# The first weights of an f32 transformer kernel: input in halves, a chain of half-sized weight transfers, constant products around the first transposes

## Chip, cores and metric

One core of one Trainium2 chip runs the whole program. The metric is the device time of the kernel in microseconds (us), the median of several executions. Everything is f32.

## What is computed

Two blocks in sequence on x, 256 tokens by 1024 features. The first block has two hybrid layers. Each of them begins with a gated feed-forward layer on the normed input, and only this beginning matters here:

```python
def rmsnorm(x, g):
    xf = x.astype(jnp.float32)
    y = xf * lax.rsqrt(jnp.mean(xf * xf, axis=-1, keepdims=True) + EPS)
    return (y * g.astype(jnp.float32)).astype(x.dtype)

def swiglu(x, w_gu, w_down):
    gate, up = jnp.split(x @ w_gu, 2, axis=-1)
    return (jax.nn.silu(gate) * up) @ w_down
```

with D_MODEL = 1024 and D_FF = 2816. After it come a mixer (a gated recurrence, windowed attention, spatial gating), a second feed-forward layer and a gated projection of p; then the same again for layer two. The second block has a short convolution, latent attention and two mixture-of-experts layers with 64 experts, whose weights are read from HBM as well. All weights are used once, 617 MB of reads in all.

## The kernel before

The program is written out by hand, one instruction stream per engine, with semaphores between them. Names that the steps below touch:

- **Weights.** `ring` has four slots of 3.1 MB in SBUF. A feed-forward layer is cut into 11 units of 256 hidden columns; unit u uses slot u % 4. One unit is three transfers of 1 MB, issued on SyncE's queue by `load` (line 1684): the gate part and the up part (`ffn_gate_up`, both 128 partitions x 8 pieces x 256 columns) and the down part (`ffn_down`). Each of them adds 16 to `unit_loaded[slot]`. Before it issues, `load` waits for `unit_free[slot]`. The first unit is issued by `load_first` (lines 1687 and 1688), without a wait; its down part counts on `final_loaded`, a semaphore of much later loads that is borrowed here. The queue's order is: two small tables (`const`, `gT1`), x (line 1678, into `h`), unit 0, units 1, 2 and 3, and then one unit each time a slot comes free.
- **Other queues.** ScalarE's queue issues ten small loads, and the second part of `const` (784 KB, line 1979) behind its first evictions. GpSimd issues nine loads (`rows`, `sgw` and others, lines 1768 to 1774; 2.53 MB) behind its first power, which follows the squares of x.
- **TensorE.** In order: a transpose of the gains (line 2649); `h_turn`, 16 transposes of x (line 2333), after a wait for all of x; a transpose of `gT2` (line 2656), the gains and convolution weights of the second block; a wait for the evictions (`h_copied`); then `ffn`. `gate_up` (line 2362) makes 128 hidden columns for all tokens in 16 products of 256 columns, eight with gate weights and eight with up weights, and waits once per unit (`loaded`, line 2349: all three parts, for unit 0 the two first). `spread` (line 2345) sets the statistics of the norm into PSUM after the first 128 columns. `down` (line 2372) is four products of 512 columns. In the profile each f32 product is two records.
- **ScalarE and VectorE.** `h_copied` evicts the transposed x with its gain: twelve activations (line 1803) and one VectorE product (line 2054). ScalarE then squares x (line 1808), VectorE and GpSimd make the reciprocal root, and VectorE multiplies each gate and up result by it (lines 2075 and 2076), ScalarE does the silu, VectorE the product (`hidden_ready`).
- `S_mla`, five semaphores, counts the loads of the latent attention in the second block. TensorE waits there for the counts in `MLA_LOADS` (line 590).

Of the kernel before, what the change touches and what calls it, by code (L numbers as in the profile page):

```python
# [27 lines left out]
P = 128  # L28
# [142 lines left out]
class Semaphores:  # L171

    def __init__(self, sem):
        self.const_loaded = sem("const_loaded")
        self.small_loaded = sem("small_loaded")
        self.h_loaded = sem("h_loaded")
        self.gl_ready = sem("gl_ready")
        self.h_half = sem("h_half")
# [81 lines left out]
        self.mla_pv = sem("mla_pv")  # L261
        self.mla_out = sem("mla_out")
        self.mla_lat_copied = sem("mla_lat_copied")
# [29 lines left out]
def build(nc, A, out):  # L293

    ctx = ExitStack()
    with ctx:
# [3 lines left out]
        S = Semaphores(lambda name: ctx.enter_context(nc.semaphore(name)))  # L300
# [5 lines left out]
        h = sb("h", [P, 3, D])  # L306
# [282 lines left out]

        MLA_LOADS = [2, 2, 2, 3, 4]  # L590

# [1083 lines left out]
        def _(sp):  # L1675
            sp.dma_start(const[:, 0:CONST_FIRST], A["const_table"][:, 0:CONST_FIRST]).then_inc(S.const_loaded, 16)
            sp.dma_start(gT1[:, :], A["norm_gains"].rearrange("l n (k c) -> (l n k) c", c=P)).then_inc(S.const_loaded, 16)
            sp.dma_start(h[:, 0:2, :], x_in).then_inc(S.h_loaded, 16)

# [6 lines left out]
            def load_first(parts):  # L1686
                for (dst, src), counted in zip(parts, (unit_loaded[0], unit_loaded[0], S.final_loaded)):
                    sp.dma_start(dst, src).then_inc(counted, 16)

# [634 lines left out]
        def _(pe):  # L2324
            mm = nc.tensor.matmul

            def h_turn(q):

                for t in range(2):
                    for n in range(2):  # L2330
                        pe.wait_ge(S.h_half, 4 * q + 2 * t + n + 1)
                        for k in range(4):
                            last = nc.tensor.transpose(PS[:, 2 * t + n, k * P:(k + 1) * P],
                                                       h[:, t, (4 * n + k) * P:(4 * n + k + 1) * P], ident)
                        last.then_inc(S.h_turned, 1)
# [12 lines left out]
            def loaded(use, slot):  # L2348
                pe.wait_ge(unit_loaded[slot], 48 * use + (48 if slot else 32))

            def ffn(l, m, u0, n, with_p=False):
                def gate_up(f, local):

                    unit = u0 + local // 2
                    slot = unit % SLOTS
                    w = ring[:, slot, 0:4096].rearrange("p (s k f) -> p s k f", s=2, k=KD)
                    j = local % 2
                    if j == 0:
                        loaded(USES * l + f[0] + unit // SLOTS, slot)
                    for s in range(2):  # L2360
                        for k in range(KD):
                            last = mm(PS[:, 4 + local % 4, s * 256:(s + 1) * 256], lhsT=w[:, s, k, j * P:(j + 1) * P],  # L2362
                                      rhs=xT[:, k, META:T2], start=k == 0, stop=k == KD - 1)
                            if s == k == 0 and j == 1 and local > 1:

                                last.then_inc(unit_free[(unit - 1) % SLOTS], 1)
                    last.then_inc(S.gateup_done, 1)
# [15 lines left out]
                gate_up([0], 0)  # L2383
                spread(n, 0)
                gate_up([0], 1)
                if m == 0:
# [263 lines left out]
            for l in range(DEPTH):  # L2650
                if l == 0:
                    pe.wait_ge(S.h_loaded, 16)
                h_turn(4 * l)
                if l == 0:
                    pe.wait_ge(S.small_loaded, SMALL_LOADS)
                    nc.tensor.transpose(PS[:, 7, 0:n_rows2], gT2[0:n_rows2, :], ident[0:n_rows2, 0:n_rows2]).then_inc(S.rowsT_done, 1)
                h_copied(4 * l)
# [36 lines left out]
```

## Time and profile before

| | us |
|---|---|
| median of 3 executions | 2574.58 |
| lowest, highest | 2574.37, 2577.57 |
| profiled execution | 2573.37 |
| its span | 2571.5 |
| TensorE busy | 2413.5 (94% of the span) |
| VectorE busy | 695.3 |
| ScalarE busy | 341.8 |
| mean granted TensorE clock | 0.979 of full speed |
| HBM traffic | 616.89 MB read, 240 GB/s over the span |

The profile is of one execution. The span runs from the first instruction to the last, and the execution's own time is 1.9 us longer. A row of a timeline has the start, the time that a merged group of instructions took, the engine, the line in the kernel, output and input, the count, and in brackets the idle time before it with what ended it. "SPq" is SyncE as an issuer of DMAs; the time in such a row is the time the issuing took, not that of the transfer. A granted clock of 1.00 is 2.4 GHz and one of 0.50 is 1.2 GHz.

### The profile page before, as it was taken

```text
span 2571.5 us, 29601 instructions
## 1 busy us (share of the span) xinstructions
PE 2413.5 (94%) x11424; PEld 1464.8 (57%) x11424; DVE 695.3 (27%) x1575; ACT 341.8 (13%) x829; POOL 48.2 (2%) x95
## 2 busy tenths in 40 slices
PE   8999999999999999999999988988989998989887
PEld 6776647775677655777576533444437553444432
DVE  1112631112211263111222432333333343233233
ACT  1101230002100123000210200000012220000001
POOL 2000000000100000000000000000000000000000
PEclk9999999999999999999999999999999999999999
DMA  9443334433644243343282399999992259999997
GB/s 318 147 148 113 128 104 161 147 119 114 236 156 160 92 148 113 135 161 131 86 301 118 131 403 422 422 422 422 422 402 101 82 237 409 422 422 422 422 422 304
DMA packets 205207, 618.88 MB, mean 241 GB/s; under 512 B 15005, under 2 KB 120294, under 8 KB 155734
## 3 DMA queue, kind: packets, MB, share of 16 engines
q1 hardware_dynamic: 198080, 610.25, 61.3%
q0 software_dynamic: 1600, 5.06, 0.6%
q10 hardware_dynamic: 5462, 2.67, 0.4%
q8 instruction: 45, 0.74, 0.1%
q14 instruction: 20, 0.16, 0.0%
HBM read 616.89 MB, written 1.05 MB: 240 GB/s over the span
## 4 chain that ended last, share of the span: by engine, by line
PE 67%; DMA 24%; DVE 3%; SPq 2%; issue 1%; ACT 1%; DVEq 0%; POOL 0%; POOLq 0%; ACTq 0%
DMA ring<-expert_parts 23%; PE PS L2362 23%; PE PS L2372 11%; PE PS L1643 6%; PE PS L1550 4%; PE PS L2414 3%; PE PS L2449 3%; PE PS L1600 2%; PE PS L2599 2%; PE PS L1620 2%; SPq L1042 2%; PE PS L2431 1%; PE PS L758 1%; PE PS L1156 1%; PE PS L623 1%
## 5 line engine op out<-in xcount | busy, mean ns | idle before, releaser
L2362 PE MATMUL PS<-xT,ring 128*128 128x256 f32 x2816 | 627.2, 381 | 7.0 <-DMA ring<-ffn_gate_up 2.9
L2362 PEld LDWEIGHTS PS<-xT,ring 128*128 128x128 f32 x2816 | 537.6, 191 | 116.1 <-issue 41.0
L1643 PE MATMUL PS<-ring,arena 128*32 128x512 f32 x2048 | 264.5, 661 | 72.8 <-DMA ring<-expert_parts 72.8
L2372 PE MATMUL PS<-ring,arena 128*128 128x512 f32 x704 | 315.9, 592 | 0.0
L1600 PE MATMUL PS<-arena,xn 128*128 128x128 f32 (+1 forms) x1536 | 271.4, 306 | 4.3 <-DVE arena L1359 4.3
L1600 PEld LDWEIGHTS PS<-arena,xn 128*128 128x128 f32 (+1 forms) x1536 | 215.4, 189 | 90.7 <-issue 31.7
L2075 DVE TENSOR_TENSOR arena<-PS,rb 128x256 f32<-128x256 f32 x88 | 37.4, 425 | 728.8 <-PE PS L2362 728.6
L1643 PEld LDWEIGHTS PS<-ring,arena 128*32 128x32 f32 x2048 | 75.4, 120 | 251.2 <-issue 251.0
L2372 PEld LDWEIGHTS PS<-ring,arena 128*128 128x128 f32 x704 | 133.5, 190 | 132.6 <-issue 126.8
L1460 DVE TENSOR_TENSOR h<-h,PS 128x1024 f32<-128x1024 f32 (+1 forms) x96 | 116.8, 1217 | 323.4 <-PE PS L1620 323.4
L1620 PE MATMUL PS<-arena 128*128 128x512 f32 (+1 forms) x404 | 198.5, 615 | 5.3 <-DVE h L1460 5.3
L1825 ACT ACTIVATE arena<-arena 128x256 f32<-128x256 f32 x88 | 36.6, 416 | 804.7 <-DVE arena L2075 804.6
L1663 PE MATMUL PS<-ring,arena 128*32 128x512 f32 x1024 | 118.2, 602 | 24.3 <-ACT arena L1281 24.3
L1620 PEld LDWEIGHTS PS<-arena 128*128 128x128 f32 (+1 forms) x404 | 56.6, 160 | 103.2 <-issue 85.5
L1550 PE MATMUL PS<-xT,ring 128*128 128x272 f32 x384 | 90.7, 398 | 1.6 <-ACT xT L1087 0.8
L2449 PE MATMUL PS<-ring,xT 128*128 128x512 f32 x192 | 87.7, 603 | 0.0
L1550 PEld LDWEIGHTS PS<-xT,ring 128*128 128x128 f32 x384 | 73.5, 193 | 18.2 <-issue 2.0
L1663 PEld LDWEIGHTS PS<-ring,arena 128*32 128x32 f32 x1024 | 30.3, 110 | 86.3 <-issue 58.8
L2414 PE MATMUL PS<-ring,xT 128*128 128x512 f32 (+1 forms) x192 | 69.6, 522 | 0.2
L1280 ACT ACTIVATE arena<-PS 128x272 f32<-128x272 f32 x32 | 12.7, 398 | 428.5 <-PE PS L1633 428.5
L1515 DVE TENSOR_TENSOR arena<-arena,PS 128x256 f32<-128x256 f32 x32 | 13.4, 420 | 184.7 <-ACT arena L1278 184.7
L1451 DVE TENSOR_SCALAR arena<-rows,arena 128x128 f32<-128x128 f32 x96 | 32.9, 343 | 107.8 <-ACT arena L1284 104.4
(381 smaller groups left out, 1707.2 us busy)
## 6 DMA issues: line engine op xcount, KB each, us to landing
ring<-expert_parts SPq DMA_DIRECT2D x384, 1024.0 KB, 15.1
ring<-ffn_gate_up SPq DMA_DIRECT2D x88, 1024.0 KB, 7.7
ring<-ffn_down SPq DMA_DIRECT2D x44, 1024.0 KB, 9.8
ring<-w_in SPq DMA_DIRECT2D x16, 768.0 KB, 5.8
ring<-conv_w_in SPq DMA_DIRECT2D x12, 1024.0 KB, 12.0
ring<-w_out_rows SPq DMA_DIRECT2D x8, 768.0 KB, 6.3
ring<-ple_gate SPq DMA_DIRECT2D x8, 768.0 KB, 6.2
rows<-norm_gains POOLq DMA_DIRECT2D x8, 512.0 KB, 8.9
```

The lines of the kernel that those rows point to most:

```text
L1042: return sp.dma_start(ring[:, j, PART * n:PART * (n + 1)], src[:, n].rearrange("o p w -> p (o w)"))
L1460: v_.tensor_tensor(tile2(h[0:w, t, :]), tile2(h[0:w, t, :]), PS[0:w, 6:8, :], ALU.add).then_inc(M[i].added, 1)
L1550: last = mm(PS[:, 3 * b + s, 0:T2], lhsT=w[:, s, k, j * P:(j + 1) * P], rhs=xT[:, k, :], start=k == 0, stop=k == KD - 1)
L1600: last = mm(PS[:, half, (k % HALF) * P:(k % HALF + 1) * P], lhsT=xn[0:w, t, k * P:(k + 1) * P], rhs=onehot[0:w, t, :], start=t == 0, stop= ...
L1620: last = mm(PS[0:w, bank + c, :], lhsT=weightsT[:, P * t:P * t + w], rhs=ysb[:, c * 512:(c + 1) * 512], start=True, stop=True)
L1643: last = mm(PS[BLK * j:BLK * (j + 1), 2, :], lhsT=xgT[:, k, j * BLK:(j + 1) * BLK], rhs=gu[j][:, k, :], start=k == 0, stop=k == KD - 1)
L1663: last = mm(PS[BLK * j:BLK * (j + 1), 4 + n, :], lhsT=hidT[:, f, j * BLK:(j + 1) * BLK], rhs=w[:, f, n * 512:(n + 1) * 512], start=f == 0, ...
L2362: last = mm(PS[:, 4 + local % 4, s * 256:(s + 1) * 256], lhsT=w[:, s, k, j * P:(j + 1) * P], rhs=xT[:, k, META:T2], start=k == 0, stop=k = ...
L2372: return mm(PS[:, 2 * t + n, :], lhsT=hid[:, j, t * P:(t + 1) * P], rhs=w[:, j, n * 512:(n + 1) * 512], start=first, stop=final, skip_grou ...
L2414: last = mm(PS[:, bank, at:at + width], lhsT=src[:, k, xcol(t)], rhs=w[:, k, 0:width], start=k == 0, stop=k == kk - 1)
L2449: last = mm(PS[:, bank, :], lhsT=xT[:, k, xcol(t)], rhs=wu[:, k, :], start=k == 0, stop=k == KD - 1)
L2599: last = mm(PS[:, 2 * t + n, :], lhsT=xT[:, k, xcol(t)], rhs=wo[:, k, :], start=k == 2, stop=k == 7)
```

## The change

x is sent as two transfers, one for each 128 tokens, with a semaphore each (`h_loaded`, `h_second`). TensorE waits for each half before its eight transposes.

The gate and up weights of the first unit are sent as four transfers of 512 KB (four of the eight pieces of the contraction each). The first is issued when the first half of x has landed, the second when the second half has, and each further one when the last but one has landed, so two of them (1 MB) are under way. The unit's down part is issued when the third quarter has landed, and unit 1 after the fourth. TensorE waits for each quarter before the products that read it, in place of one wait for gate and up. The four quarters count on four of the `S_mla` semaphores, and the counts in `MLA_LOADS` are raised to match. An unused semaphore goes.

`first_warm(2)` sets two products of a constant with the identity, whose results nobody reads, ahead of the transposes of x, and two more behind them. The transpose of `gT2` moves from ahead of the first products to behind `spread`.

```diff
-        MLA_LOADS = [2, 2, 2, 3, 4]
+        MLA_LOADS = [3, 3, 3, 4, 4]
...
-            sp.dma_start(h[:, 0:2, :], x_in).then_inc(S.h_loaded, 16)
+            sp.dma_start(h[:, 0:1, :], x_in[:, 0:1, :]).then_inc(S.h_loaded, 16)
+            sp.dma_start(h[:, 1:2, :], x_in[:, 1:2, :]).then_inc(S.h_second, 16)
...
             def load_first(parts):
-                for (dst, src), counted in zip(parts, (unit_loaded[0], unit_loaded[0], S.final_loaded)):
-                    sp.dma_start(dst, src).then_inc(counted, 16)
+
+                (gate, gate_src), (up, up_src), (dn, dn_src) = parts
+                sp.wait_ge(S.h_loaded, 16)
+                sp.dma_start(gate[:, 0:4], gate_src[:, 0:4]).then_inc(S_mla[0], 16)
+                sp.wait_ge(S.h_second, 16)
+                sp.dma_start(gate[:, 4:8], gate_src[:, 4:8]).then_inc(S_mla[1], 16)
+                sp.wait_ge(S_mla[0], 16)
+                sp.dma_start(up[:, 0:4], up_src[:, 0:4]).then_inc(S_mla[2], 16)
+                sp.wait_ge(S_mla[1], 16)
+                sp.dma_start(up[:, 4:8], up_src[:, 4:8]).then_inc(S_mla[3], 16)
+                sp.wait_ge(S_mla[2], 16)
+                sp.dma_start(dn, dn_src).then_inc(S.final_loaded, 16)
+                sp.wait_ge(S_mla[3], 16)
...
+            def first_warm(n):
+
+                for _ in range(n):
+                    mm(PS[:, 5, 0:2 * P], lhsT=ident, rhs=const[:, 0:2 * P], start=True, stop=True)
+
             def h_turn(q):
 
                 for t in range(2):
+                    if q == 0:
+                        pe.wait_ge(S.h_second if t else S.h_loaded, 16)
...
-                pe.wait_ge(unit_loaded[slot], 48 * use + (48 if slot else 32))
+                pe.wait_ge(unit_loaded[slot], 48 * use + (48 if slot else 0))
...
-                    if j == 0:
+                    if j == 0 and (m or local):
                         loaded(USES * l + f[0] + unit // SLOTS, slot)
                     for s in range(2):
                         for k in range(KD):
+                            if m == local == 0 and k in (0, 4):
+                                pe.wait_ge(S_mla[2 * s + k // 4], 16)
...
                 gate_up([0], 0)
                 spread(n, 0)
+                if m == 0:
+                    pe.wait_ge(S.small_loaded, SMALL_LOADS)
+                    nc.tensor.transpose(PS[:, 7, 0:n_rows2], gT2[0:n_rows2, :], ident[0:n_rows2, 0:n_rows2]).then_inc(S.rowsT_done, 1)
...
                 if l == 0:
-                    pe.wait_ge(S.h_loaded, 16)
+                    first_warm(2)
                 h_turn(4 * l)
                 if l == 0:
-                    pe.wait_ge(S.small_loaded, SMALL_LOADS)
-                    nc.tensor.transpose(PS[:, 7, 0:n_rows2], gT2[0:n_rows2, :], ident[0:n_rows2, 0:n_rows2]).then_inc(S.rowsT_done, 1)
+                    first_warm(2)
                 h_copied(4 * l)
```

How the instructions stand on SyncE's queue at the start of the program, before (`mla_loaded0` to `3` are the first four of `S_mla`):

```order
L1676 DMA const<-const_table 128x264
L1677 DMA gT<-norm_gains 128x128
L1678 DMA h<-x 128x2x1024
L1688 DMA ring<-ffn_gate_up 128x8x256 x2
L1688 DMA ring<-ffn_down 128x2x1024
L1684 DMA ring<-ffn_gate_up 128x8x256 [waits unit_free1]
L1684 DMA ring<-ffn_gate_up 128x8x256
```

and in the changed kernel:

```order
L1678 DMA h<-x 128x1024
L1679 DMA h<-x 128x1024
L1691 DMA ring<-ffn_gate_up 128x4x256 [waits h_loaded]
L1693 DMA ring<-ffn_gate_up 128x4x256 [waits h_second]
L1695 DMA ring<-ffn_gate_up 128x4x256 [waits mla_loaded0]
L1697 DMA ring<-ffn_gate_up 128x4x256 [waits mla_loaded1]
L1699 DMA ring<-ffn_down 128x2x1024 [waits mla_loaded2]
L1685 DMA ring<-ffn_gate_up 128x8x256 [waits unit_free1,mla_loaded3]
L1685 DMA ring<-ffn_gate_up 128x8x256
```

Unit 0's gate and up parts have become four issues, each behind a landing, and unit 1 has moved behind the landing of the last of them. Before, nothing on this queue waited for a landing.

TensorE from the transposes of x to unit 1, before:

```order
L2333 MATMUL PS<-const,h 128x128 x3
L2656 MATMUL PS<-const,gT 128x73 [waits small_loaded]
L2362 MATMUL PS<-xT,ring 128x256 [waits unit_loaded0,xT_vec,xT_act]
L2362 MATMUL PS<-xT,ring 128x256 x15
L2345 MATMUL PS<-diag,const 128x128 [waits diag_ready]
L2345 MATMUL PS<-diag,const 128x128
L2362 MATMUL PS<-xT,ring 128x256 x16
L2372 MATMUL PS<-ring,arena 128x512 [waits hidden_ready,final_loaded]
```

and in the changed kernel:

```order
L2342 MATMUL PS<-const 128x256 x2
L2383 MATMUL PS<-xT,ring 128x256 [waits mla_loaded0,xT_vec,xT_act]
L2383 MATMUL PS<-xT,ring 128x256 x3
L2383 MATMUL PS<-xT,ring 128x256 [waits mla_loaded1]
L2383 MATMUL PS<-xT,ring 128x256 x3
L2383 MATMUL PS<-xT,ring 128x256 [waits mla_loaded2]
L2383 MATMUL PS<-xT,ring 128x256 x3
L2383 MATMUL PS<-xT,ring 128x256 [waits mla_loaded3]
L2383 MATMUL PS<-xT,ring 128x256 x3
L2364 MATMUL PS<-diag,const 128x128 [waits diag_ready]
L2364 MATMUL PS<-diag,const 128x128
L2408 MATMUL PS<-const,gT 128x73 [waits small_loaded]
```

The 16 products of the first 128 columns have four waits instead of one, the transpose of `gT2` (128x73) stands behind the statistics instead of ahead of the products, and two constant products stand where it was.

## Rows read from the trace of the kernel before

**Rows 1.** Timeline of TensorE, start of the program

```profile
7.03 3.67 PE L2333 MATMUL PS<-const,h 128*128 128x128 f32 x16 [3.07 <-DMA h<-x]
10.50 0.33 PE L2656 MATMUL PS<-const,gT 73*128 73x73 f32 x1
13.74 8.83 PE L2362 MATMUL PS<-xT,ring 128*128 128x256 f32 x32 [2.91 <-DMA ring<-ffn_gate_up]
22.41 0.61 PE L2345 MATMUL PS<-diag,const 128*128 128x128 f32 x4
...
29.76 3.60 PE L2372 MATMUL PS<-ring,arena 128*128 128x512 f32 x8
34.91 7.17 PE L2362 MATMUL PS<-xT,ring 128*128 128x256 f32 x32 [1.55 <-DMA ring<-ffn_down]
...
45.35 7.07 PE L2362 MATMUL PS<-xT,ring 128*128 128x256 f32 x32
```

**Rows 2.** Timeline of SyncE's queue: x, units 0, 1 and 2

```profile
1.64 0.43 SPq L1678 DMA_DIRECT2D h<-x  x1
2.11 1.09 SPq L1688 DMA_DIRECT2D ring<-ffn_gate_up  x2
...
7.07 6.05 SPq L1684 DMA_DIRECT2D ring<-ffn_gate_up  x2
13.16 4.75 SPq L1684 DMA_DIRECT2D ring<-ffn_down  x1
...
31.09 3.74 SPq L1684 DMA_DIRECT2D ring<-ffn_down  x1
```

**Rows 3.** Single DMAs issued at 0.72, 1.64, 2.62, 7.07, 13.16, 31.09: us to landing

```profile
const<-const_table SPq DMA_DIRECT2D x1, 132.0 KB, 2.3
...
h<-x SPq DMA_DIRECT2D x1, 1024.0 KB, 5.3
...
ring<-ffn_gate_up SPq DMA_DIRECT2D x1, 1024.0 KB, 11.0
...
ring<-ffn_gate_up SPq DMA_DIRECT2D x1, 1024.0 KB, 20.2
...
ring<-ffn_down SPq DMA_DIRECT2D x1, 1024.0 KB, 21.7
...
ring<-ffn_down SPq DMA_DIRECT2D x1, 1024.0 KB, 12.4
```

**Rows 4.** Chain of work that ended last, 0 to 200 us, in order of time

```profile
42.08 3.43 PE PS L2372 x8
45.52 6.91 PE PS L2362 x32
```

**Rows 5.** Stretches: length, busy PE, PEld, DVE, ACT, POOL, granted clock, DMA share, GB/s

```profile
0.00:7.00 7.00, 0.48 (x1) 0.18 (x1) 0.35 (x2) 1.28 (x1) 0.19 (x4) 1.00 0.74 217
7.00:16.00 9.00, 6.06 (x25) 5.40 (x26) 1.34 (x4) 5.28 (x16) 2.18 (x4) 0.93 1.08 364
16.00:34.90 18.90, 17.36 (x70) 13.27 (x68) 3.13 (x9) 0.83 (x2) 7.41 (x18) 0.94 1.05 364
```

**Rows 6.** DMA queues of GpSimd (q0) and ScalarE (q10), 0 to 60 us: packets, MB, share

```profile
q0 software_dynamic: 800, 2.53, 12.2%
q10 hardware_dynamic: 582, 0.91, 4.2%
```

**Rows 7.** Timeline of VectorE, its eviction of x

```profile
10.74 0.69 DVE L2054 TENSOR_TENSOR xT<-PS,gT 128x512 f32<-128x512 f32 x1 [6.45 <-PE PS L2333]
```

**Rows 8.** Stretches with the clock down, and one after the wait of 1.55 us

```profile
14.80:18.20 3.40, 3.40 (x10) 2.65 (x9) 0.24 (x2) 0.00 (x0) 3.40 (x6) 0.50 1.01 387
35.00:45.00 10.00, 10.00 (x40) 7.50 (x41) 1.18 (x3) 0.42 (x1) 6.32 (x19) 1.00 1.08 364
653.10:659.90 6.80, 6.08 (x14) 4.88 (x15) 1.39 (x4) 3.76 (x7) 4.04 (x7) 0.50 1.07 374
```

**Rows 9.** Timeline of TensorE, start of the second layer

```profile
651.67 1.32 PE L2333 MATMUL PS<-const,h 128*128 128x128 f32 x8 [2.50 <-DVE h L2035]
```

More of the change, by code:

```diff
@@ L177, in __init__ @@
         self.h_loaded = sem("h_loaded")
+        self.h_second = sem("h_second")
         self.gl_ready = sem("gl_ready")
@@ L261, in __init__ @@
         self.mla_pv = sem("mla_pv")
-        self.mla_out = sem("mla_out")
         self.mla_lat_copied = sem("mla_lat_copied")
```

## The prediction

> **What bounds the kernel now.** I read the engines' shares of the span first (in the table above), then TensorE's timeline of the first 60 us with SyncE's queue beside it, the landing times of single DMAs, the bytes moved in stretches, and last the stretches in which the clock was down. TensorE is busy 94% of the span. From 34.91 us on it runs a beat of 6.91 + 3.43 = 10.34 us per 128 hidden columns without a stop [rows 1, 4]. So a shift of 34.91 reaches the end of the program one for one, and a shift of anything earlier counts only as far as it moves 34.91. What sets it?
>
> TensorE starts unit 0 at 13.74, when the up weights have landed (issued near 2.6, 11.0 us under way), works until 29.76 + 3.60 = 33.36, and then stands 1.55 us for unit 1's third part: issued at 13.16, 21.7 us under way, landed at 34.87 [rows 1 to 3]. That landing is a matter of bytes, not of when it was asked for. Up to 34.9 us the engines moved 1.52 + 3.28 + 6.88 = 11.68 MB, with a DMA share of 1.05 to 1.08 in the last two stretches [rows 5]. SyncE's queue had to bring 0.2 (tables) + 1.05 (x) + 3.15 (unit 0) + 3.15 (unit 1) = 7.54 MB; beside it run 2.53 MB of GpSimd's queue and 0.91 of ScalarE's [rows 6], which the change leaves as they are. That makes 10.98 MB; the other 0.7 belong to unit 2, queued behind. Unit 2 lands at 31.09 + 12.4 = 43.5 and is wanted at 45.35 + 10.34 = 55.7 [rows 1 to 4]. Only unit 1 binds.
>
> **The new start, part by part.** x as a whole takes 5.3 us from 1.64 [rows 2, 3]; its second half is 0.52 MB, 1.4 us at 364 GB/s [rows 5], so the first half lands at about 5.5, the second at 6.9. A link of the new chain (0.52 MB, asked for when an earlier one has landed) isn't in this trace. The row below it is 132 KB in 2.3 us, the row above it the 5.3 us of x [rows 3]. I take 3.6: the 2.3 us, less 0.2 for its own 135 KB, plus 1.4 for 0.52 MB at 364 GB/s, and 0.1 for the queue to wake, since with 1 MB under way little stands ahead of a link. Then gate's halves land at 9.1 and 10.5, up's at 12.7 and 14.1, and unit 1 is first asked for at about 14.2 instead of 7.07 [rows 2].
>
> TensorE: the 16 transposes (3.67 us) run from 5.5 to 9.2. The evictions end 4.4 us after the first transpose, as now (7.03 to 10.74 + 0.69 [rows 1, 7]), at 9.9. Of the four constant products, 0.43 us each (6.91 us for 16 of that width [rows 4]), the first two lie in the wait for x and the other two beside the evictions, ending at 10.1; without those covers they would cost 1.7 us. Then 1.7 us of products per half: gate until 13.5, up's first half until 15.2, the second until 16.9. The statistics (0.61 us) and the moved transpose (0.33) make 17.9 [rows 1], the second 128 columns 24.8, the down products 28.2. With the clock down as long as now (3.4 us at half [rows 8], 1.7 us lost) it is 29.9. **TensorE is ready for unit 1 at 28.2 to 29.9**, 3.5 to 5.2 us before 33.36. Unit 0's down part, asked for at 12.8, is wanted at 24.8. If it takes the 20.2 us of unit 1's first part [rows 3] it lands at 33.0, and TensorE is ready at 36.4, 1.1 us after unit 1; with x's 5.3 us it costs nothing. I take nothing, since its bytes stand ahead of all of unit 1's; 1.1 us is a bound. VectorE's wait for the moved transpose is 0.3 us; behind it stands only the first hidden block, covered by 6.9 us of products. The counts in the later loads follow the reused semaphores: nothing.
>
> **What it is worth is decided at unit 1.** Its landing needs the same 10.98 MB. Asking in small pieces can't bring them sooner on full engines; it can only leave gaps. By 14.2 us SyncE's queue has brought 3.35 MB and ScalarE's 0.91. Unit 0's down part is then just starting and GpSimd's rows start about 1.5 us sooner than now (their issue follows the squares of x), so I put 4.65 MB at 16 us against 4.80 [rows 5]. The 0.15 MB missing are 0.4 us at 364 GB/s: **unit 1 at 35.3, +0.4**. Lower end: the 0.7 MB of unit 2 no longer run ahead, -1.9. Upper end: each link takes 5.3 us, two pairs of them put unit 1's request 3.4 us later, and little fills the gap: +2.9.
>
> TensorE will then stand 5 to 7 us before unit 1, where it stood 1.55. After that 1.55 us the clock stayed at 2.4 GHz (35 to 45 at 1.00). After the stand from 10.8 to 13.74 it was at 1.2 GHz from 14.8 to 18.2; at 650, after a stand of 2.50 us and another short one, from 653.1 to 659.9 [rows 1, 8, 9]. Half of 3.4 and of 6.8 us is lost, 1.7 or 3.4 us. Here nothing later hides it, since unit 2 has 12 us to spare. Bounds are 0 and 3.4. A stand of 5 to 7 us is like the rows with a fall, and dense work after it like the one at 14.8, so I take 2.0. The fall that now lies at 14.8 gives nothing back where it is avoided: what it delays ends at 33.36, ahead of unit 1.
>
> Sum: +0.4 + 2.0 = **+2.4 us**. The profiled execution took 2573.37 us and would take 2575.8. It lies 1.2 us under the median of the three, 2574.58, so the forecast for a median is **2577.0**. A measurement of this kernel can tell about 0.2%, 5.1 us, from no change.
>
> A rule speaks against halves. The Trainium skill (DMA: Bandwidth & Descriptors, Rules for kernel authors) asks for at least 1 MiB per DMA, and its table in Bandwidth has 341 GB/s at 1 MB and 138 at 64 KB. By it I estimate some 300 GB/s for 512 KB, 0.3 us more per link and so +0.6 on the sum. No run shows it yet.
>
> **Rivals.**
> (a) *The wait eats the gain and nothing else happens*: the clock stays up; 0 to +0.8 us, 2574.6 to 2575.4. For it: the 1.55 us without a fall. Against: the stand is three times that. 15%.
> (b) *Fewer bytes of unit 2 run ahead*, as unit 1's parts are asked for close together: up to -1.9 us, 2572.7. Against: the queue is as deep as now by then. 8%.
> (c) *The early start goes through*: unit 1 gets ahead of GpSimd's 2.53 MB and TensorE goes on at 28.2 to 29.9, 5.0 to 6.7 us sooner, 2567.9 to 2569.6. It decides if unit 1 lands by 29.8. With all the bytes that takes 6.3 MB in 13.8 us, 459 GB/s where the row has 364 [rows 5]. 3%.
> (d) *The chain starves the engines*, the slower side: links at 5.3 us, because the 0.91 MB of ScalarE's queue and GpSimd's rows come in between while SyncE's queue holds only 1 MB; unit 1 at 37.8, the clock down for 6.8 us: +2.9 + 3.4 = +6.3, 2580.9. It passes 5.1 us when unit 1 lands after 36.6 with the long fall. Under way beside GpSimd's rows a part took 20.2 us [rows 3], which speaks for it; that ScalarE's table is small, against. 12%. The Trainium skill (DMA: Bandwidth & Descriptors, Queues, rings and completion order) says that the engines go round robin between queues, by which a short queue would lose its share.
> (e) *x's halves don't land apart*, both at 6.9: TensorE's start moves by 1.4 us, unit 1 by some 0.4. Inside the forecast's range.
>
> **How the numbers follow.** The forecast with (e) has 62%, 2575 to 2579. The range of 8 in 10 takes in (a), most of (b) and the shorter end of (d): 2573.0 to 2580.4. Faster by over 0.2%: (c) and little else, 4%. Slower by over 0.2%: three quarters of (d), 9%. Within: 87%.
>
> **What would show it.** Right: first products of unit 0 near 10 us and the last of its first up products near 17; one wait of over 4 us that a DMA of unit 1 ends at 35 to 36; a granted clock of 0.50 for some us behind it; 11.7 MB moved by then; the beat of 10.34 us as before. Wrong: no long wait before unit 1, or its landing before 33.5; a clock of 1.00 after it. A DMA share well under 1 between 7 and 15 us would speak for (d).

## The result, and the profile after

The change made the kernel slower: 2583.12 us against 2574.47 us, medians of 16 executions each. The ratio is 1.0031 with an interval of 1.0020 to 1.0042, +5.1 to +10.8 us. I had forecast 2577.0, at most 2580.4, and had given 9% to slower by over 0.2%. A second measurement of the same kernel, below, has 2581.48 against 2576.44, ratio 1.0023 (1.0009 to 1.0037). A ratio is not the quotient of the two medians beside it and can differ from it by 0.001. One of the 35 executions of the kernel before beside e9 to e12 took 8001.73 us at a mean granted clock of 0.305 and is left out of the ratios (the median without it is 2576.26).

The profiled execution took 2584.11 us, span 2582.3. TensorE's timeline of its start, against [rows 1]:

```profile
6.91 3.67 PE L2352 MATMUL PS<-const,h 128*128 128x128 f32 x16 [1.25 <-DMA h<-x]
...
11.74 3.62 PE L2383 MATMUL PS<-xT,ring 128*128 128x256 f32 x16
17.53 5.41 PE L2383 MATMUL PS<-xT,ring 128*128 128x256 f32 x16 [2.17 <-DMA ring<-ffn_gate_up]
...
30.24 3.60 PE L2393 MATMUL PS<-ring,arena 128*128 128x512 f32 x8
38.77 8.80 PE L2383 MATMUL PS<-xT,ring 128*128 128x256 f32 x32 [4.94 <-DMA ring<-ffn_down]
...
50.84 7.07 PE L2383 MATMUL PS<-xT,ring 128*128 128x256 f32 x32
```

The transposes start 0.12 us sooner than before, not 1.5. The gate products begin at 11.74, two us sooner than 13.74, but the up products only at 17.53, and TensorE is ready for unit 1 at 33.84, later than the 33.36 of before. Unit 1 lands at 38.7 instead of 34.9. The first 32 records behind it take 8.80 us instead of 7.17.

SyncE's queue in the same profile, against [rows 2]:

```profile
1.64 0.42 SPq L1678 DMA_DIRECT2D h<-x  x1
2.10 0.43 SPq L1679 DMA_DIRECT2D h<-x  x1
6.89 0.38 SPq L1691 DMA_DIRECT2D ring<-ffn_gate_up  x1
8.19 0.38 SPq L1693 DMA_DIRECT2D ring<-ffn_gate_up  x1
10.42 0.37 SPq L1695 DMA_DIRECT2D ring<-ffn_gate_up  x1
13.06 0.37 SPq L1697 DMA_DIRECT2D ring<-ffn_gate_up  x1
17.50 0.37 SPq L1699 DMA_DIRECT2D ring<-ffn_down  x1
18.88 5.42 SPq L1685 DMA_DIRECT2D ring<-ffn_gate_up  x2
24.34 5.78 SPq L1685 DMA_DIRECT2D ring<-ffn_down  x1
```

Each issue from 6.89 to 18.88 follows a landing. The first half of x landed after 5.2 us, about as long as the whole of x took [rows 3]; the second after 6.1. Single DMAs of the chain, issued at 6.89, 8.19, 10.42 and 13.06, with KB and us to landing:

```profile
ring<-ffn_gate_up SPq DMA_DIRECT2D x1, 512.0 KB, 3.5
...
ring<-ffn_gate_up SPq DMA_DIRECT2D x1, 512.0 KB, 4.8
...
ring<-ffn_gate_up SPq DMA_DIRECT2D x1, 512.0 KB, 7.1
...
ring<-ffn_gate_up SPq DMA_DIRECT2D x1, 512.0 KB, 5.8
```

I had put every link (one transfer of the chain, from issue to landing) at 3.6. The stretches, with the columns of [rows 5], then two single microseconds and the stretch behind unit 1's landing:

```profile
0.00:7.00 7.00, 2.27 (x6) 1.38 (x7) 0.35 (x2) 1.28 (x1) 0.19 (x4) 1.00 0.64 189
7.00:16.00 9.00, 8.36 (x36) 7.36 (x36) 1.34 (x4) 5.28 (x16) 2.31 (x4) 1.00 0.85 261
16.00:34.90 18.90, 16.30 (x61) 12.29 (x61) 3.10 (x9) 0.83 (x2) 6.89 (x16) 0.91 1.04 348
6.00:7.00 1.00, 0.09 (x1) 0.09 (x2) 0.00 (x0) 0.00 (x0) 0.00 (x0) 1.00 0.39 119
7.00:8.00 1.00, 1.00 (x5) 1.00 (x6) 0.00 (x0) 0.00 (x0) 0.00 (x0) 1.00 0.11 34
38.90:42.10 3.20, 3.20 (x8) 2.57 (x9) 0.00 (x0) 0.00 (x0) 2.42 (x8) 0.50 1.10 353
```

By 16 us 1.32 + 2.35 = 3.67 MB have moved, where it was 4.80 [rows 5]. The 1.13 MB missing are 3.1 us at 364 GB/s, and the stretch to 34.9 runs at 348 instead of 364 GB/s, 0.3 MB or 0.8 us more. Together that is the 3.9 us by which unit 1 is late. Counted up to the start of unit 1's products, both kernels have moved the same 11.67 MB, 8.22 of them on SyncE's queue, before by 34.9 us and now by 38.7. Between 6 and 8 us the DMA engines are nearly idle: x's halves land at 6.9 and 8.2, and until the first of them nothing new is asked for. Against the 364 and 378 GB/s of before these two microseconds account for 0.59 of the 1.13 MB; the rest is missing from 8 to 16 us, where 289 GB/s stand against 362. Then the clock is at 1.2 GHz behind the stand (TensorE's wait ahead of unit 1), which costs 1.6 us.

So 5.5 us of the 10.8 between the spans of the two profiled executions arise in the first 50 us, and they stay. The first transposes after the first feed-forward layer, of the kernel before and of the changed one:

```profile
246.04 1.32 PE L2333 MATMUL PS<-const,h 128*128 128x128 f32 x8 [0.63 <-DVE h L2035]
```

```profile
251.53 1.32 PE L2352 MATMUL PS<-const,h 128*128 128x128 f32 x8 [0.63 <-DVE h L2047]
```

I call this time the mark; it contains the whole start and little else. The rest of the 10.8, 5.3 us, comes far behind the change. In both kernels the clock falls where the first expert layer begins, but for 10 us in the profile of before and 20 in that of the changed kernel:

```profile
1458.70:1468.80 10.10, 10.10 (x28) 6.50 (x26) 0.91 (x2) 0.00 (x0) 0.00 (x0) 0.50 1.01 423
```

```profile
1465.50:1485.90 20.40, 20.21 (x52) 11.69 (x51) 2.64 (x3) 0.16 (x1) 0.00 (x0) 0.50 0.64 266
```

Whether the change causes that too was the second question for the runs.

### The profile page after: what moved, and what is told of

It reads as the page before. It is cut to its first block, busy times and chain, and to the rows that moved or that the text cites. A ratio compares the mean times of both kernels' runs of the same rounds, so it can differ in the third digit from the quotient of the medians.

```text
span 2582.3 us, 29622 instructions
## 1 busy us (share of the span) xinstructions
PE 2422.9 (94%) x11432; PEld 1470.4 (57%) x11432; DVE 695.3 (27%) x1575; ACT 341.5 (13%) x829; POOL 48.1 (2%) x95
## 4 chain that ended last, share of the span: by engine, by line
PE 67%; DMA 24%; DVE 3%; SPq 2%; issue 1%; ACT 1%; DVEq 0%; POOL 0%; POOLq 0%; ACTq 0%
DMA ring<-expert_parts 23%; PE PS L2383 23%; PE PS L2393 11%; PE PS L1643 6%; PE PS L1550 4%; PE PS L2438 3%; PE PS L2473 3%; PE PS L1600 2%; PE PS L2623 2%; PE PS L1620 2%; SPq L1042 2%; PE PS L758 1%; PE PS L2455 1%; PE PS L1156 1%; PE PS L623 1%
## 5 line engine op out<-in xcount | busy, mean ns | idle before, releaser
L1837 ACT ACTIVATE arena<-arena 128x256 f32<-128x256 f32 x88 | 36.6, 416 | 809.1 <-DVE arena L2087 809.1
```

## The experiments

The twelve runs fall into three groups, e1 to e4, e5 to e8 and e9 to e12. Each group ran on one chip with the kernel before beside it: 12 executions of each kernel (10 of e2, e5 and e6), 35 of the kernel before. A version with a second number repeats an earlier one. In the table "asked" is the issue of unit 1's first part, "unit 1" the start of its products, "stand" TensorE's wait ahead of it, "rest" the span behind the mark, all from the run's one profile. Where "stand" is 0, unit 1 had landed before TensorE was ready.

| run | asked | unit 1 | stand | mark | rest | median, before | ratio (interval) |
|---|---|---|---|---|---|---|---|
| before | 7.07 | 34.91 | 1.55 | 246.04 | 2325.5 | | |
| changed | 18.88 | 38.77 | 4.94 | 251.53 | 2330.8 | 2583.12, 2574.47 | 1.0031 (1.0020, 1.0042) |
| e1 no chain | 7.42 | 35.33 | 6.48 | 248.24 | 2326.0 | 2576.68, 2576.15 | 1.0012 (0.9995, 1.0028) |
| e2 tail free | 13.98 | 39.12 | 4.46 | 251.69 | 2323.4 | 2577.66, 2576.15 | 1.0015 (0.9999, 1.0032) |
| e3 constants in the stand | 18.80 | 38.86 | 2.52 | 249.99 | 2326.9 | 2579.89, 2576.15 | 1.0011 (0.9995, 1.0027) |
| e4 GpSimd's loads late | 17.80 | 31.34 | 0.25 | 242.47 | 2322.3 | 2570.72, 2576.15 | 0.9976 (0.9962, 0.9989) |
| e5 table late | 16.83 | 39.45 | 9.70 | 252.78 | 2320.8 | 2582.19, 2574.80 | 1.0027 (1.0007, 1.0046) |
| e6 three under way | 12.92 | 37.22 | 7.08 | 250.77 | 2321.0 | 2578.03, 2574.80 | 1.0010 (0.9992, 1.0028) |
| e7 before, loads late | 9.16 | 35.05 | 0 | 246.07 | 2332.9 | 2574.49, 2574.80 | 1.0002 (0.9986, 1.0018) |
| e8 no chain, loads late | 7.79 | 29.83 | 0 | 240.85 | 2331.9 | 2573.36, 2574.80 | 0.9990 (0.9972, 1.0007) |
| e9 changed, again | 20.54 | 38.75 | 4.00 | 252.28 | 2320.9 | 2581.48, 2576.44 | 1.0023 (1.0009, 1.0037) |
| e10 no constants | 21.30 | 38.71 | 4.49 | 251.22 | 2333.1 | 2581.38, 2576.44 | 1.0025 (1.0008, 1.0043) |
| e11 as e4, again | 18.79 | 33.66 | 0 | 244.68 | 2327.5 | 2573.98, 2576.44 | 0.9985 (0.9970, 1.0001) |
| e12 no chain, both late | 7.65 | 28.60 | 0 | 239.62 | 2322.8 | 2566.59, 2576.44 | 0.9963 (0.9949, 0.9977) |

**e1: without the chain.** All six waits of `load_first` go; halves, constants and the moved transpose stay.

```diff
-                sp.wait_ge(S.h_loaded, 16)
                 sp.dma_start(gate[:, 0:4], gate_src[:, 0:4]).then_inc(S_mla[0], 16)
-                sp.wait_ge(S.h_second, 16)
                 sp.dma_start(gate[:, 4:8], gate_src[:, 4:8]).then_inc(S_mla[1], 16)
-                sp.wait_ge(S_mla[0], 16)
...
```

> The changed kernel with all six waits of the SyncE queue in the first unit's load taken away: x in halves, gate and up in halves, the constant products and the moved transpose stay, and the waits of TensorE for each quarter. Theory 1 (the chain leaves the DMA engines short of work: 3.67 MB moved by 16 us instead of 4.80, so unit 1 lands 3.9 us later, and the longer stand before it costs a fall of the clock): 4.7 to 4.8 MB by 16 us, unit 1 lands at 34.5 to 35.3, TensorE ready before 33, no or a short stand, 2572 to 2576. Theory 2 (the added products, the moved transpose or the many small pieces cost, not the waits): unit 1 still lands after 37 or the time stays above 2580.

Its stretches and TensorE's timeline:

```profile
0.00:7.00 7.00, 3.33 (x11) 2.44 (x12) 0.36 (x2) 1.28 (x1) 0.19 (x4) 1.00 0.70 224
7.00:16.00 9.00, 8.32 (x41) 6.79 (x39) 1.34 (x4) 5.28 (x16) 3.37 (x6) 1.00 1.08 361
16.00:34.90 18.90, 12.85 (x53) 9.55 (x53) 3.10 (x9) 0.83 (x2) 6.51 (x17) 0.93 1.05 364
```

```profile
5.84 3.12 PE L2346 MATMUL PS<-const,h 128*128 128x128 f32 x16 [0.21 <-DMA h<-x]
...
25.25 3.60 PE L2387 MATMUL PS<-ring,arena 128*128 128x512 f32 x8
35.33 8.96 PE L2377 MATMUL PS<-xT,ring 128*128 128x256 f32 x32 [6.48 <-DMA ring<-ffn_down]
```

4.82 MB by 16 us, as before (4.80), and unit 1 at 35.3. Theory 1 holds for the bytes and the landing: the waits made unit 1 late, not the halves. Its "no or a short stand" was missed: TensorE was ready at 28.85 and stood 6.48 us. This run is what I had worked out for the changed kernel: TensorE ready in time (28.2 to 29.9 forecast), unit 1 at 35.33 (35.3), a long stand and a fall of the clock (8.96 instead of 7.17 us). Its mark is +2.2 us (forecast +2.4). TensorE is ready for unit 1 4.5 us sooner, and none of it reaches the mark. Theory 2 falls. By the median alone, 0.5 us over its before with a ratio's interval of -1.3 to +7.2 us, this run could not have told it.

**e2: only the last two waits gone**, those ahead of the down part and ahead of unit 1.

```diff
                 sp.dma_start(up[:, 4:8], up_src[:, 4:8]).then_inc(S_mla[3], 16)
-                sp.wait_ge(S_mla[2], 16)
                 sp.dma_start(dn, dn_src).then_inc(S.final_loaded, 16)
-                sp.wait_ge(S_mla[3], 16)
```

> The changed kernel with only the last two waits of the SyncE queue taken away (those ahead of unit 0's down part and ahead of unit 1); the four quarters are still a chain, and the last of them is issued at about 13, so unit 1 is asked for at about 14 instead of 18.9. Theory 1: the bytes missing by 13 us stay missing (about 0.6 MB, 1.7 us), the rest of the loss goes: unit 1 lands at 36 to 37, 2575 to 2580. Theory 1b (only the late request of unit 1 matters): it lands at 35 or before. Theory 2: nothing moves, 38 or later.

```profile
13.98 9.01 SPq L1685 DMA_DIRECT2D ring<-ffn_gate_up  x2
```

```profile
39.12 8.62 PE L2381 MATMUL PS<-xT,ring 128*128 128x256 f32 x32 [4.46 <-DMA ring<-ffn_down]
```

Unit 1 is asked for at 13.98, 4.9 us sooner, and lands at 39.1, no sooner at all. I had expected 36 to 37. By 16 us it has moved 3.61 MB, as little as the changed kernel, which fits. But from 16 to 34.9 it moves 371 GB/s and gains back 0.4 MB, and up to the landing some 12.1 MB have moved instead of 11.7, 8.69 instead of 8.22 of them on SyncE's queue. The surplus can only belong to unit 2, whose first parts SyncE issued at 28.7; why that got a share ahead of unit 1's last part isn't shown. Together with the other profiles of the full chain this settles the request: asked for at 13.98, 18.80, 18.88, 20.54 and 21.30 (e2, e3, changed, e9, e10), unit 1 starts between 38.7 and 39.1 in all five. When it is asked for decides nothing; the bytes missing before that stay missing.

**e3: constant products in the stand ahead of unit 1.**

```diff
                 down([0], 0, first=True)
+                if m == 0:
+                    for _ in range(10):
+                        mm(PS[:, 6, 0:2 * P], lhsT=ident, rhs=const[:, 0:2 * P], start=True, stop=True)
```

> The changed kernel with ten more constant products (0.43 us each, 4.3 us) on TensorE ahead of its wait for unit 1, where it stands 4.9 us. Unit 1's landing doesn't change (38.7). If the fall of the clock behind the stand is a cost of its own, as I put it at 2.0 us, the clock stays at 1.00 behind unit 1 and the products of that unit take 7.1 us instead of 8.8: 1.7 us less at 50 us, and about 2 us less in all (2581). Rival: the clock falls all the same, or the products delay the real ones, and nothing is gained.

```profile
31.86 4.48 PE L2415 MATMUL PS<-const 128*128 128x256 f32 x20
38.86 7.17 PE L2383 MATMUL PS<-xT,ring 128*128 128x256 f32 x32 [2.52 <-DMA ring<-ffn_down]
```

The clock stays up after a stand of 2.52 us, unit 1's records take 7.17 us instead of 8.80, and the mark is at 249.99, 1.5 us sooner at the same landing. So the fall was a term of its own, 1.6 us, where I had put 2.0. Against the before of its own group this median is +3.7 us, where the changed kernel had +8.7 and, in e9, +5.0; the direction fits, and the size lies within the intervals.

**e4 and e11: GpSimd's nine loads behind its first tables**, in the changed kernel.

```diff
                 power(n0, rsh, msh, 2)
+                if l == 0:
+                    first_tables(pool)
                 for i in range(4):
                     nc_.dma_start(rows[:, i, :], ...
...
-                if l == 0:
-                    first_tables(pool)
```

> The changed kernel with GpSimd's nine loads (2.53 MB) behind its first tables, that is after about 60 us instead of at 14 to 20. Theory 1 says the landing of unit 1 is a matter of bytes: without 2.53 MB it lands 6 to 7 us sooner, at 32, before TensorE is ready (33.8), the stand and the fall of the clock go, and the time is 2575 or less. If instead the chain's latency or the count of requests sets it, unit 1 lands at 36 or later and the time stays above 2578.

```profile
31.34 7.17 PE L2383 MATMUL PS<-xT,ring 128*128 128x256 f32 x32 [0.25 <-DMA ring<-ffn_down]
```

Unit 1 lands 7.4 us sooner, by the 7.0 us that 2.53 MB take at 364 GB/s and a little more. By then 9.13 MB have moved, the 11.67 of the changed kernel less GpSimd's 2.53; SyncE's queue has brought 8.20 of them, as there. The fall is gone and the stand is down to 0.25 us, and the kernel is faster than both. That shows that bytes set the landing.

> The changed kernel with GpSimd's loads behind its tables, once more: its first measurement (2570.7, ratio 0.9976) was faster than both kernels, and faster than the one without the chain (2573.4) although that one started unit 1 1.5 us sooner. If the start decides, it comes out 3 to 4 us under the kernel before; if the first measurement was right as it stands, 6 us.

The repetition is 2.5 us under its before (0.9985, interval 0.9970 to 1.0001) where the first was 5.4 under; I had put 3 to 4 if the start decides, and 6 if the first measurement was right as it stood. Its mark is 244.68: unit 1 landed at 32.6, the clock fell in unit 0 and TensorE was ready only at 33.66, with no stand behind to hide that. The two agree within their intervals, and what I take as the gain is what the two marks show against the 246.04 of before: 1.4 and 3.6 us. The 2.2 us between these two profiles of one kernel are also what a single mark can be off by.

**e5: ScalarE's 784 KB table late**, behind its second silu.

```diff
                 if m == 0:
+                    act.dma_start(const[:, CONST_FIRST:], A["const_table"][:, CONST_FIRST:]).then_inc(S.const2_loaded, 16)
...
                 h_copied(4 * l, 64 * l)
-                if l == 0:
-                    act.dma_start(const[:, CONST_FIRST:], A["const_table"][:, CONST_FIRST:]).then_inc(S.const2_loaded, 16)
```

> The changed kernel with ScalarE's 784 KB table (issued at 9.8, beside the links of the chain) behind its second silu, some 34 us. The links for up's halves took 7.1 and 5.8 us where I had put 3.6. If they are long because the table shares the engines with them, they take about 4, unit 1 is asked for at 16 or before instead of 18.9, and unit 1 lands at 36 or before (the table's 0.8 MB is gone from ahead of it too, 2.2 us). If they are long by themselves (each waits for its slowest engine), they stay at 5 to 7 and unit 1 lands at 36 to 37, by the table's bytes alone.

The links of the chain for up's halves, issued at 9.75 and 12.02:

```profile
ring<-ffn_gate_up SPq DMA_DIRECT2D x1, 512.0 KB, 4.5
...
ring<-ffn_gate_up SPq DMA_DIRECT2D x1, 512.0 KB, 4.8
```

With the table beside them the third link took 7.1 us and the fourth 5.8; in e9 it was 7.6 and 8.5. So the table makes the third at least 2.6 us longer and the fourth 1.0 or more. The rest, 4.5 and 4.8 us against my 3.6, is there without it. Unit 1 still lands at 39.45, although asked for at 16.83: the second silu came at 26.8, not 34, so that the table's bytes still went ahead of unit 1, and the expectation for the landing was missed by my own edit. Its stand of 9.70 us is the longest of all, as TensorE was ready 4 us sooner. The median is 7.4 us above its before, no better than the changed kernel.

**e6: three halves under way instead of two.** Each wait moves one issue down.

```diff
-                sp.wait_ge(S.h_loaded, 16)
                 sp.dma_start(gate[:, 0:4], gate_src[:, 0:4]).then_inc(S_mla[0], 16)
-                sp.wait_ge(S.h_second, 16)
+                sp.wait_ge(S.h_loaded, 16)
                 sp.dma_start(gate[:, 4:8], gate_src[:, 4:8]).then_inc(S_mla[1], 16)
-                sp.wait_ge(S_mla[0], 16)
+                sp.wait_ge(S.h_second, 16)
...
                 sp.dma_start(dn, dn_src).then_inc(S.final_loaded, 16)
-                sp.wait_ge(S_mla[3], 16)
+                sp.wait_ge(S_mla[2], 16)
```

> The changed kernel with three halves (1.5 MB) under way instead of two: the first half of gate goes out behind x without a wait, each further part waits for the last but two. If the loss is engines standing idle between links, most of it goes: DMA share near 1 between 7 and 16, 4.5 MB or more moved by 16 us, unit 1 lands at 36 or before. If the form of the chain (any wait for a landing) is what costs, it lands at 37.5 or later.

```profile
7.00:16.00 9.00, 9.00 (x40) 8.19 (x39) 1.34 (x4) 5.28 (x16) 2.79 (x5) 1.00 0.95 324
```

4.51 MB by 16 us, DMA share 0.95: half a megabyte more under way gives back 0.84 of the 1.13 MB, 0.49 of them between 6 and 8 us, where gate's first half had been asked for without a wait. Unit 1 lands at 37.2, 1.6 us sooner than in the changed kernel, yet above the 36 expected; the 0.29 MB still missing and the 351 GB/s up to 34.9 account for 1.5 of the remaining 2.3 us, and 0.8 stay open.

**e7: the same late loads in the kernel before**, as a control for e4; the edit is the diff of e4.

> The kernel before with GpSimd's nine loads (2.53 MB) behind its first tables and nothing else changed. Bytes set the landing of unit 1: it comes near 28 instead of 34.9, and TensorE, ready at 33.4, doesn't stand; unit 1 starts at 33.4, 1.5 us sooner than before, and sooner or later than the changed kernel with the same edit (31.3) by 2 us. Time 2572 to 2574. If this kernel came out as fast as that one (2570.7), the early start of the change would be worth nothing even there.

```profile
9.11 3.47 PE L2333 MATMUL PS<-const,h 128*128 128x128 f32 x16 [4.69 <-DMA h<-x]
```

No gain: 2574.49 against 2574.80. Unit 1 lands at 28.6, as expected. But in this profile x lands at 9.1 instead of 7.0, 2.1 us late with nothing changed ahead of it, so that TensorE is ready at 35.05 and the 1.5 us are used up. With x at 7.0 it would have been 33.0, by my estimate. The median doesn't decide it, since 1.5 us lie inside its interval of -3.6 to +4.6 us.

**e8: no chain, loads late**, the edits of e1 and e4 together.

> The change without the six waits of the SyncE queue, and GpSimd's loads behind its tables. TensorE is ready for unit 1 at 28.7 (as in the run without the chain) and unit 1 lands at 28 to 29 (35.3 less 6 to 7 us): no stand, no fall of the clock, unit 1 starts near 29, 6 us sooner than in the kernel before. Time 2567 to 2570, faster than both kernels and than the run with the chain and late loads. Rival: the landing stays above 31 and the gain stops at 3 us.

Unit 1 has landed at 27.9, its products start at 29.83 when TensorE is ready, and the mark is 5.2 us ahead of before; I had expected some 29 and 6, so the start is one us short. The median is only 1.4 us ahead of its before (interval -7.2 to +1.8), 3.4 us above what I expected: a miss by the time more than by the start.

**e9: the changed kernel again**, with no edit, for the question of the rest.

> The changed kernel once more, unaltered. Its first measurement was 8.65 us above the kernel before (interval 5.2 to 10.8), while in its profile the start alone is 5.5 us late (first transposes after the first feed-forward layer at 251.53 instead of 246.04), and the rest came behind 1439 us with a longer stretch of low clock. Theory A (the start is all of it, the rest is where the falls of the clock happened to lie): a difference near 5 to 6 us, and in the new profile the same lateness at the start with another remainder. Theory B (the change also causes later falls): again 8 us or more, and a mean granted clock at least 0.002 under that of the kernel before.

```profile
38.75 9.58 PE L2383 MATMUL PS<-xT,ring 128*128 128x256 f32 x32 [4.00 <-DMA ring<-ffn_down]
...
252.28 1.32 PE L2352 MATMUL PS<-const,h 128*128 128x128 f32 x8 [0.62 <-DVE h L2047]
```

The start is as late as in the first profile, +6.2 us at the mark, but the rest is 2320.9 us, 9.9 us shorter than in the first profile and 4.6 shorter than that of before. The 20 us at 1.2 GHz at the first expert layer are 10 this time. Over the fourteen profiles the rest lies between 2320.8 and 2333.1, without order: 2332.9 stands in e7, whose start is that of before, and 2331.9 in e8, with one of the quickest. The clock accounts for all of it. Behind the mark, the time that TensorE's clock takes away (one less the granted clock, summed over stretches of 10 us) is 47 to 63 us in the fourteen profiles, and the rest less this sum is 2270 to 2274 us in every one: 2272.5 before, 2271.3 and 2273.5 in the two profiles of the changed kernel. So the change adds no work or wait behind the mark; what remains is whether it moves falls of the clock. Theory A holds: medians 5.0 us apart, ratio +5.9 us. Of theory B's sign, a mean granted clock 0.002 under before, about half is there (0.9766 against 0.9777), which the fall behind unit 1 accounts for in part (2.4 us, as in this profile, are 0.0009). Whether the change also shifts later falls by a microsecond or two on average stays open.

**e10: without the four constant products.**

```diff
             for l in range(DEPTH):
-                if l == 0:
-                    first_warm(2)
                 h_turn(4 * l)
-                if l == 0:
-                    first_warm(2)
                 h_copied(4 * l)
```

> The changed kernel without its four constant products. They lie in waits: the landing of unit 1 is late with or without them, so the start is as late as with them (unit 1 at 38 to 39, 251 to 252 at the first transposes after the first layer) and the time within 2 us of the changed kernel. Rival: without them the clock falls during the first unit, and TensorE is ready later; that would still be ahead of unit 1. A difference of more than 3 us either way would mean that they cost or save something I don't see.

Unit 1 starts at 38.71, the mark is 251.22, the median 2581.38 beside the 2581.48 of e9 in the same group. They cost and save nothing that can be seen here, as I had costed them.

**e12: no chain, and both GpSimd's loads and ScalarE's table late**, the edits of e1, e4 and e5 together.

> The change without the six waits of the SyncE queue, GpSimd's loads behind its tables, and ScalarE's 784 KB table behind its second silu: nothing but x and the weights on the DMA engines in the first 34 us. TensorE was already not waiting for unit 1 in the version with only GpSimd's loads late, so the start gains little more: unit 1 begins at 28.5 to 30, the first transposes after the first layer are at 240 to 241, 5 to 6 us sooner than in the kernel before, and so is the end, if nothing waits for the table later (VectorE needs the rotary tables only in the mixer).

```profile
28.60 7.07 PE L2376 MATMUL PS<-xT,ring 128*128 128x256 f32 x32
...
239.62 1.32 PE L2345 MATMUL PS<-const,h 128*128 128x128 f32 x8 [0.62 <-DVE h L2040]
```

The fastest version: 2566.59 against 2576.44, ratio 0.9963 (0.9949 to 0.9977), faster than the kernel before and than the changed one. TensorE goes from unit 0 into unit 1 without a stand and without a fall of the clock. Mark and start are at the quick end of what I expected: the mark is 6.4 us ahead, and the interval of the time, -5.9 to -13.1 us, takes that in, though the median is 9.9 us ahead.

## Why the prediction was wrong

**What binds.** Right. That only unit 1's landing reaches the end and that it is a matter of bytes is shown by e4 (2.53 MB away, 7.4 us sooner) and by the two kernels themselves (11.67 MB moved at either landing). That it isn't a matter of the request is shown by e2, asked for 4.9 us sooner and landed no sooner. TensorE's own start matters only once those bytes are away: e8 and e12. Nothing for unit 0's down part was right too: it landed at 28.0 and was wanted at 30.24.

**The early start of TensorE.** Too early by 0.3 to 1.4 us. "The first half lands at about 5.5, the second at 6.9": the transposes, which wait for the first half, began at 5.84 to 6.58 in the three versions without the chain (e1, e8, e12) and at 6.03 to 6.91 in those with it, e9 and the changed kernel being the same program. So this moves from execution to execution, and no effect of the chain on x is shown. In the changed kernel's profile the halves landed at 6.9 and 8.2, apart, but both 1.3 to 1.4 us late; rival (e) had the first of these dates, not the second.

**The step that failed: "I put 4.65 MB at 16 us against 4.80", and so "+0.4" for the landing.** Measured were 3.67 MB and +3.9 us (in e9 3.95 MB and +3.8). It was built on two dates of the chain. The first link went out at 6.9 instead of 5.5, and up to 8.2 only one was under way; the two microseconds from 6 to 8 are half of the missing bytes. And "I take 3.6" for a link: measured were 3.5, 4.8, 7.1 and 5.8 us. I had built that from the landing of a small transfer plus its bytes at full rate, as if a link had all DMA engines to itself. It shares them with the other link and with the table (e5: at least 2.6 and 1.0 us of it), and a share of 0.9 or less in several microseconds from 8 to 16 says that some engines had nothing to do meanwhile; which ones isn't shown. Unit 1 was asked for at 18.9 instead of 14.2, but by e2 that date alone cost nothing: the bytes did.

Two checks on my own numbers would have warned me. By my dates, four links and the table, 2.9 MB, had to move between 6.9 and 14.1 us, 403 GB/s where [rows 5] has 364 for full engines. And the 132 KB that I took off the small transfer are 0.4 us at that rate, not 0.2, so that the link should have come out at 3.4, still further off. My upper end, +2.9, was too low as well: I had bounded a link by the 5.3 us of x, ahead of which only two small tables stood, though [rows 3] holds 20.2 us for a part that shared the engines, and I had reckoned it by the date of the request.

**The clock.** Right: a stand of 4.94 us, 3.2 us at 1.2 GHz, 1.6 us lost where I had 2.0, shown as a separate term by e3. In e9 it was 4.8 us of work at the lower clock, 2.4 us lost. Landing and fall make up the mark: 3.9 + 1.6 = 5.5 us in the first profile, 3.8 + 2.4 = 6.2 in e9.

**The rivals.** It went as (d), which I gave 12%: the chain starves the engines, unit 1 after 36.6. Its mechanism is shown by the bytes missing at 16 us and by e1, which has them back. Its price, 6.3 us, is close to the marks of +5.5 and +6.2 partly by luck: it was 2.9 for the landing and 3.4 for the clock, where 3.9 and 1.6 were measured (2.4 in e9), so two errors of about one us and more cancel. I had held against it that "ScalarE's table is small". Of my signs the long wait, the clock of 0.50 and the 11.7 MB came; the first gate products (11.7 instead of 10), the end of the first up products (22.9 instead of 17) and the landing (38.7 instead of 35 to 36) didn't, and the DMA share of 0.85 from 7 to 16 us is the sign that I had named for (d). The argument for giving it more was in my own text: if full engines can't be made faster by asking in pieces, the only thing a chain can change is to leave gaps.

**The rule on sizes.** The Trainium skill (DMA: Bandwidth & Descriptors, Rules for kernel authors) asks for 1 MiB per DMA, and I had estimated 0.6 us from its table. The Trainium skill's table (same page, Bandwidth) was measured with transfers issued from GpSimd, and these go out on SyncE's queue. e1 sends the same halves, with 1 MB parts behind them, at 361 GB/s between 7 and 16 us, where the 1 MB parts alone had 364: here the size cost nothing that can be seen, and the waiting for landings 3.9 us. That the engines go round robin between queues (the Trainium skill, DMA: Bandwidth & Descriptors, Queues, rings and completion order) agrees with e5, where a link is 2.6 us shorter without the table beside it; that they share is shown by this, in which order isn't.

## What to carry to other kernels

At the start of a kernel, ask which landing binds and count the bytes that must be through before it, on all queues: moving 2.53 MB that nobody needs yet behind it brought that landing 7.4 us sooner here (e4), but the mark moved only as far as TensorE was ready for it, against the kernel before from nothing (e7) to 5.2 us (e8). Sending the urgent bytes in order, without a wait between them, cost the engines nothing. A chain of transfers that wait for each other's landing is paid in idle engines: between 7 and 16 us the DMA share was 0.85 with 1 MB under way, 0.95 with 1.5 MB (e6) and 1.08 without the waits (e1). Price a link by a transfer that shared the engines in the trace, not by a lone one, and check that the bytes of all links fit the rate that full engines had. Compare such edits by a time shortly behind them: two profiles of one kernel differed at the mark by 0.7 us (the changed kernel and e9) and by 2.2 (e4 and e11), where twelve executions of one kernel and 35 of the other leave some 4 us of doubt. So one profile tells 5 us, not 2, and where two terms are read apart, as landing and fall in e1, the terms say more than the sum.

## What was unexpected in the hardware

x's landing moves by itself. The first half, 512 KB, took 5.2 us in the first profile of the changed kernel and 4.3 in e9, the same program; the whole, 1024 KB, took 5.3 us before and 7.4 in e7, with the same requests ahead of it. So the half wasn't surely quicker than the whole in a single profile. Whether work queued behind it matters isn't shown: 4.2, 4.9 and 4.5 us with it (e1, e8, e12). In the changed kernel the engines were at a share of 0.39 and 0.11 in the two microseconds before the second half landed at 8.2, so nearly all of its bytes seem to have been through before; that one or a few engines came late is my reading, not shown.

The time follows the mean granted clock closely with an unchanged program: the sixteen executions of the changed kernel run from 2575.4 us at 0.979 to 2592.3 at 0.971. Behind the mark the clock took 47 to 63 us, depending on the profile, and what is left of the rest agrees within 4 us over all fourteen profiles. The beginning of the first expert layer alone was at 1.2 GHz for 10 us in one execution and 20 in another.
